# Four V projections among the first attention units, with an earlier order of turns and packed gate columns

## The chip, the cores and the metric

The kernel runs on one core of a Trainium2 chip. The metric is the device time of one execution in microseconds (us), the median of several runs. The profile is one further execution, taken by the hardware profiler. TensorE (PE) multiplies matrices, VectorE (DVE), ScalarE (ACT) and GpSimd (POOL) do the elementwise work, SyncE (SP) issues most of the DMAs. Each engine runs its own instruction stream in order; semaphores hold one stream back for another.

## The reference, cut to what matters

One decoder block on 1024 tokens of width 1024, all in float32, with 32 experts behind it:

```
h = rms_norm(x, norm_attn_g)
proj = h @ w_in                      # 3080 columns, split into:
da_q, da_k, da_v, ml_qk, ml_v, ml_o, ml_g = split(proj)
a_out = diff_attention(da_q, da_k, da_v, rel_bias_table, lam)   # 4 heads, causal
qk = silu(causal_conv(ml_qk)); gates = ml_g + mlstm_gate_b      # 4 input, 4 forget gates
m_out = mlstm_chunkwise(q, k, ml_v, log_i, log_f)               # 4 heads
m_out = head_rms_norm(m_out) * sigmoid(ml_o + mlstm_o_b)
x = x + concat(a_out, m_out) @ w_out
x = x + moe(rms_norm(x))             # top 4 of 32 experts
out = rms_norm(x, final_norm_g)
```

## The kernel before

The tokens are cut into NT = 8 tiles of 128. The kernel has five hand-written streams, one for each engine; the order of work on an engine is the order in which its code stands, and every wait is a semaphore.

**Turning x.** Each tile of x is squared (ScalarE), scaled (VectorE, L1202), turned in eight transposes on TensorE (`turn_x`, L574) and multiplied by the gain on VectorE into `hT` (L1216). Two pairs of PSUM banks alternate, so turn t waits for the gain of turn t - 2; VectorE scales tile t + 1 ahead of the gain of tile t.

**Projections.** `outs` lists 50 projections, each one bank of 128 x 512 and eight accumulating matmuls (16 passes of TensorE): QKM (8, the mLSTM's q and k), GATE (2, one for each half of the tokens, 36 columns of weights), MV (8), MO (8), Q (8), K (8), V (8). `project(o)` (L599) issues one, `take_out(o)` on ScalarE evacuates it, `proj_done` and `proj_evac` count them. Up to MO they rotate over banks 0 to 3. TensorE runs `turn_x` 0 to 3, projections 0 to 3, `turn_x` 4 to 7, the turn of the small vectors (L613), the relative-bias row (L616), and then projections 4 to 17.

**Gate rows.** The gates are scanned on VectorE (L1242) while MV runs. ScalarE computes their exponential (`em_ready`, L1036) behind its evacuation of the last MV. TensorE then transposes these rows (L625), and ahead of each of the eight MO projections it spreads half of one head's row over 128 partitions (L631, banks 6 and 7), which ScalarE copies into `m_wide`. ScalarE makes the sigmoids of the convolved q and k behind MO 4 to 7.

**mLSTM.** Eight chunks, one for each tile. Chunk t on TensorE: `ml_sums(t)` (L675, L678), a projection, `ml_chunk_state(t)` (L663), the turn of the chunk before (L686), `ml_scores(t + 1)` (L651, L655), and two more projections. So three of the 24 projections Q, K and V stand in each chunk. They and the turns share banks 6 and 7. `ml_scores(0)` stands behind all of MO. VectorE weighs scores and keys, forms queries (L1329), and divides.

**Attention.** 32 units (tile t, head h). In step u TensorE issues the transposes of unit u - 2 (L745), the logits of unit u (`da_logit`, L723, two row groups of 64 partitions), and the values of unit u - 2 (L756). Softmax runs on VectorE (L1400 to L1417) and ScalarE (L1095). In steps 4 and 6 TensorE turns the experts' bias tables (`turn_biases`, L772), from step 8 on there are output projections (L783). Banks 5 and 7 are a ring for all but the attention's own results.

**Queue of SyncE.** In its stream, `proj_done` of the last V is waited for; behind that stand the loads of the first half of w_out (over V's weights, L364), of the two bias tables `b_gu_rows` and `b_down_rows` (over `hT`, L365 and L366), of the second half of w_out (L368) and of x (L371).

**Experts.** 32 experts follow, with 4 slots of weights streamed from HBM (L923). The diff does not touch them.

Of the kernel before, what the change touches and what calls it, by code (L numbers as in the profile page):

```python
# [27 lines left out]
ACT = mybir.ActivationFunctionType  # L28
AX = mybir.AxisListType.X

P = 128
# [52 lines left out]
def build(nc, x, norm_attn_g, w_in, rel_bias_table, lambda_q1, lambda_k1, lambda_q2, lambda_k2,  # L84
# [16 lines left out]
    with ExitStack() as ctx:  # L101
# [97 lines left out]
        gd_scaled = sb("gd_scaled", [P, DAH])  # L199
        gate_bias = sb("gate_bias", [64, 1])  # L200
        neg_half = sb("neg_half", [P, NT])
# [88 lines left out]
        QKM, Q, K, V, MV, MO, GATE = range(7)  # L290
        outs = [(QKM, h, m) for h in range(2) for m in range(4)] + [(GATE, 0, 0), (GATE, 1, 0)]
        outs += [(MV, 0, t) for t in range(NT)]
# [11 lines left out]
        first_shared = after_group[MO]  # L304
        shared = []
# [3 lines left out]
        out_bank = {o: o % 4 for o in range(first_shared)}  # L309
        out_bank.update({n: 6 + j % 2 for j, (what, n) in enumerate(shared) if what == "out"})  # L310
        turn_bank = {n: 6 + j % 2 for j, (what, n) in enumerate(shared) if what == "turn"}
# [11 lines left out]
        N_SMALL = 6 + 2  # L323
        RING, END_RING = (5, 7), (0, 1, 2, 3)
        ring, ring_bank = [], {}
        ring_read = {"ml": ml_mixed, "bias": b_ready, "mix": da_mixed, "half": x1_ready,
                     "h2": h2T_ready, "logits": logits_read, "place": place_read}
# [239 lines left out]
        def _(pe):  # L567
# [10 lines left out]
            def project(o):  # L578
                kind, a, b = outs[o]
                ps_bank = bank(out_bank[o])  # L580
                if kind < 6:
                    pe.wait_ge(group_in[kind], 16)
                if kind in (QKM, Q, K, MO, GATE):
                    pe.wait_ge(hT_ready, 4 * a + 4)
                if 4 <= o < first_shared:
                    pe.wait_ge(proj_evac, o - 3)
                elif o == 0:
                    pe.wait_ge(vec_ready, 1)
                if kind == GATE:
                    pe.wait_ge(gate_w_in, 32)  # L590
                for k in range(KD):
# [28 lines left out]

            pe.wait_ge(em_ready, 1)
            pe.wait_ge(consts, 5)
            for n, row in enumerate((row_c, row_b)):
                for t in range(NT):
                    ins = pe.transpose(bank(4)[:, 32 * n + 4 * t:32 * n + 4 * t + 4], row[:, P * t:P * t + P],  # L625
                                       ident[0:MLH, 0:MLH])
            ins.then_inc(cols_ps, 1)
            for n, o in enumerate(range(after_group[MV], after_group[MO])):
# [4 lines left out]
                project(o)  # L633

            def share(j):

                if j < 2:
                    pe.wait_ge(wide_ready, 7 + j)
# [48 lines left out]

            pe.wait_ge(qk_done, 4)
            pe.wait_ge(proj_evac, first_shared)  # L690
            pe.wait_ge(v_ones, 1)
            ml_scores(0)
            for j, (what, n) in enumerate(shared):
                t = (n - first_shared) // 3 if what == "out" else n + 1
                step_out = n - first_shared - 3 * t
                if what == "out" and step_out == 0:
                    ml_sums(t)
                    share(j)
                    project(n)
                    if t < NT - 1:  # L700
                        ml_chunk_state(t)
                elif what == "turn":
                    share(j)
                    ml_turn(n, bank(turn_bank[n]))
                else:
                    if step_out == 1 and t + 1 < NT:
                        ml_scores(t + 1)
# [97 lines left out]
            def place(t):  # L805
# [154 lines left out]
        def _(act):  # L960
# [13 lines left out]
            for ap, row, n in ((norm_ffn_g, V_GF, 8), (diff_norm_g, V_GD, 4),  # L974
# [4 lines left out]
            act.wait_ge(gate_bias_clear, 1)  # L979
            act.dma_start(gate_bias[0:4, :], mlstm_gate_b[:, 0:4].rearrange("l (g o) -> (l g) o", o=1)) \  # L980
               .then_inc(small_in, 16)
            act.dma_start(gate_bias[32:36, :], mlstm_gate_b[:, 4:8].rearrange("l (g o) -> (l g) o", o=1)) \
               .then_inc(small_in, 16)
            act.dma_start(table[:, :], rel_bias_table).then_inc(table_in, 16)
# [11 lines left out]
            def take_out(o):  # L996
# [8 lines left out]
                elif kind == GATE:  # L1005
                    ins = act.activation(gate_rows[0:36, cols], ps[0:36, :], ACT.Identity, bias=gate_bias[0:36, :])
                elif kind == Q:
# [28 lines left out]
            act.activation(row_b, row_b, ACT.Exp, scale=-1.0).then_inc(em_ready, 1)  # L1036
            for n, o in enumerate(range(after_group[MV], after_group[MO])):
# [3 lines left out]
                take_out(o)  # L1041
                if n >= 4:
                    act.wait_ge(conv_done, n - 3)
                    act.activation(ml_raw[:, n - 4, :], ml_qk[:, n - 4, :], ACT.Sigmoid).then_inc(sig_done, 1)

            act.wait_ge(lam_ready, 1)
            act.activation(lam[:, 2:4], lam[:, 0:2], ACT.Exp).then_inc(lam_exp, 1)

# [23 lines left out]

            act.wait_ge(ml_fade_in, 1)
            act.activation(ml_fade[:, :, :], ml_fade[:, :, :], ACT.Exp).then_inc(ml_fade_ready, 1)
            ml_exp(0)
            ml_exp(1)
            for t in range(NT):
                if t + 1 < NT:
                    ml_fade_q(t + 1)
                if t + 2 < NT:  # L1080
                    ml_exp(t + 2)
                take_out(first_shared + 3 * t)
                if t < NT - 1:
                    ml_square(t)
                take_out(first_shared + 3 * t + 1)
                take_out(first_shared + 3 * t + 2)

# [23 lines left out]
            for u in range(len(da_units) + 2):  # L1111
# [81 lines left out]
        def _(dve):  # L1193
# [327 lines left out]
            for u in range(3, N_UNITS + 1):  # L1521
                t = u // 4 - 2
                if u in (5, 7):
                    take_biases(u // 2 - 2)
                if u % 4 == 0 and t >= 0:
# [184 lines left out]
```

## Time and profile before

| | us |
|---|---|
| median of 3 runs | 2460.75 (2460.61 to 2462.6) |
| the profiled execution | 2460.42 |
| its span, first to last instruction | 2458.7 |
| TensorE busy | 2332.1 (95%) |
| VectorE busy | 764.3 (31%) |
| ScalarE busy | 609.6 (25%) |

### The profile page before, as it was taken

Reading aid. Unit: us, or ns where it says so; the run is one execution under the profiler, and the core shown is the slowest. Engines: PE = TensorE matmul, PEld = TensorE weight load, DVE = VectorE, ACT = ScalarE, POOL = GpSimd, SP = SyncE. Lnnn points to the kernel's source line nnn. Section 1 sums busy time; section 2 is a strip of 40 time slices with the busy share of each in tenths; the row PEclk is TensorE's granted clock in tenths of the full one; section 3 lists DMA queues with packets and bytes.
Section 4 is the critical chain, followed back from the end, with each engine's and each line's share of the span. In section 5 each row is a group of like instructions: output and inputs, shape, how many; then the busy total and the mean of one; then the engine's idle time right before and its main releaser. Section 6 shows DMA issues by size and latency. Waiting matters only on the chain.

```text
span 2458.7 us, 41234 instructions
## 1 busy us (share of the span) xinstructions
PE 2332.1 (95%) x15394; PEld 1994.0 (81%) x15395; DVE 764.3 (31%) x1819; ACT 609.6 (25%) x1284; POOL 250.5 (10%) x227
## 2 busy tenths in 40 slices
PE   7999999899969999989999999999999999999994
PEld 3343545456649999989999999999999999999994
DVE  2161321477752232222323222321222222222222
ACT  2112111244402222222222222211221222222223
POOL 1000000021130111001011101100100000010011
PEclk8999999899979999999999999999999999999997
DMA  7000000211146899869889889975976788798686
GB/s 283 35 0 0 1 0 35 101 52 53 44 141 219 271 293 287 278 214 276 280 277 298 265 261 293 296 220 183 290 241 207 215 266 251 240 286 276 208 255 217
DMA packets 440328, 485.95 MB, mean 198 GB/s; under 512 B 23965, under 2 KB 417357, under 8 KB 440252
## 3 DMA queue, kind: packets, MB, share of 16 engines
q1 hardware_dynamic: 419996, 450.33, 56.1%
q0 software_dynamic: 20080, 34.88, 6.7%
q8 instruction: 28, 0.46, 0.1%
q10 hardware_dynamic: 208, 0.16, 0.0%
q14 instruction: 16, 0.13, 0.0%
HBM read 473.41 MB, written 49.58 MB: 213 GB/s over the span
## 4 chain that ended last, share of the span: by engine, by line
PE 93%; issue 2%; DVE 2%; DMA 1%; ACT 1%; POOL 0%; SPq 0%; ACTq 0%; POOLq 0%; DVEq 0%
PE PS L923 64%; PE PS L599 14%; PE PS L783 5%; PE PS L884 2%; PE PS L866 2%; PE PS L723 1%; PE PS L756 1%; PE PS L745 1%; PE PS L675 1%; PE PS L678 0%; PE PS L802 0%; DVE unit L1400 0%; PE PS L631 0%; DMA out_dram<-unit 0%; PE PS L574 0%
## 5 line engine op out<-in xcount | busy, mean ns | idle before, releaser
L923 PE MATMUL PS<-pairA,unit 128*128 x12288 | 1588.1, 291 | 25.9 <-issue 23.3
L923 PEld LDWEIGHTS PS<-pairA,unit 128*128 128x128 f32 x12288 | 1561.7, 191 | 45.0 <-issue 34.5
L599 PE MATMUL PS<-pairA,unit 128*128 128x512 f32 (+1 forms) x544 | 245.4, 609 | 2.5 <-issue 2.5
L1646 DVE TENSOR_SCALAR unit<-PS,cur_b 128x256 f32<-128x256 f32 x256 | 112.1, 479 | 368.4 <-PE PS L923 353.5
L1178 ACT ACTIVATE unit<-PS,cur_b 128x256 f32<-128x256 f32 x256 | 107.5, 471 | 457.0 <-PE PS L923 457.0
L599 PEld LDWEIGHTS PS<-pairA,unit 128*128 128x128 f32 (+1 forms) x544 | 101.9, 191 | 138.2 <-issue 137.6
L1165 ACT ACTIVATE unit<-unit 128x512 f32<-128x512 f32 x128 | 80.6, 630 | 482.1 <-DVE unit L1646 470.0
L1169 ACT ACTIVATE unit<-PS,cur_b 128x256 f32<-128x256 f32 x256 | 107.5, 471 | 321.4 <-PE PS L923 321.4
L517 POOL DMA_INDIRECT unit<-h_dram,cur_x x66 | 69.5, 1053 | 1011.1 <-DVE cur_x L1640 994.6
L1653 DVE TENSOR_SCALAR unit<-unit 128x512 f32<-128x512 f32 x128 | 54.7, 427 | 344.8 <-ACT unit L1169 344.8
L536 POOL DMA_INDIRECT acc_dram<-pairA,cur_y x66 | 105.9, 1604 | 531.7 <-ACT pairA L1149 521.0
L1638 DVE COPY cur_b<-b_all 128x24 f32 x32 | 5.7, 178 | 436.0 <-ACT unit L1178 433.8
L1651 DVE TENSOR_TENSOR unit<-unit 128x512 f32<-128x512 f32 x128 | 88.7, 693 | 89.1 <-ACT unit L1165 89.1
L599 PE MATMUL PS<-unit,pairA 128*128 128x512 f32 x256 | 111.4, 594 | 0.2 <-ACT unit L1015 0.2
L599 PEld LDWEIGHTS PS<-unit,pairA 128*128 128x128 f32 x256 | 48.1, 190 | 60.0 <-issue 59.2
L1655 DVE SCALAR_TENSOR_TENSOR pairA<-unit 128x512 f32<-128x512 f32 x128 | 88.6, 693 | 4.4
L1616 DVE TENSOR_TENSOR pairA<-PS,vec 128x512 f32<-128x512 f32 x132 | 81.9, 682 | 0.4 <-PE PS L866 0.3
L1149 ACT ACTIVATE pairA<-PS,g_now 128x512 f32<-128x512 f32 x132 | 80.3, 700 | 6.6 <-PE PS L884 6.6
L866 PE MATMUL PS<-ident,unit 128*128 128x128 f32 x384 | 48.7, 278 | 19.7 <-DMA unit<-h_dram,cur_x 19.7
L1095 ACT ACTIVATE unit<-unit,small 128x128 f32<-128x128 f32 (+7 forms) x64 | 49.4, 772 | 54.4 <-DVE small L1403 51.0
L866 PEld LDWEIGHTS PS<-ident,unit 128*128 128x128 f32 x384 | 44.7, 144 | 20.0 <-issue 19.8
L783 PE MATMUL PS<-unit,pairA 128*128 128x512 f32 x128 | 58.4, 599 | 0.0
(228 smaller groups left out, 1245.2 us busy)
## 6 DMA issues: line engine op xcount, KB each, us to landing
unit<-in_expert_w_gu_dram SPq DMA_DIRECT2D x256, 1024.0 KB, 5.3
unit<-in_expert_w_down_dram SPq DMA_DIRECT2D x128, 1024.0 KB, 6.7
unit<-in_w_in_dram SPq DMA_DIRECT2D x6, 2048.0 KB, 14.5
pairB<-in_x_dram SPq DMA_DIRECT2D x16, 512.0 KB, 9.9
unit<-in_w_out_dram SPq DMA_DIRECT2D x2, 2048.0 KB, 12.0
h_dram<-pairA SPq DMA_DIRECT2D x8, 512.0 KB
acc_dram<-pairB SPq DMA_DIRECT2D x8, 512.0 KB
pairB<-acc_dram SPq DMA_DIRECT2D x8, 512.0 KB, 6.4
```

Of the source, the lines that this page charges most:

```text
L536: pool.indirect_dma_start(out=acc_dram, out_offset=bass.IndirectOffsetOnAxis(ap=cur_y[:, b:b + 1], axis=0), in_=y_rows[:, b, :], in_offset ...
L599: ins = pe.matmul(ps, lhs, rhs, start=(k == 0), stop=(k == KD - 1))
L783: ins = pe.matmul(ps, (da_mixT, ml_mixT)[k // 4][:, k % 4, P * t:P * t + P], w_o[k // 4][:, k % 4, HALF * half:HALF * half + HALF], start= ...
L866: ins = pe.transpose(bank(4 + q)[:, 256 * k + P * b:256 * k + P * b + P], xg[:, b, P * (2 * q + k):P * (2 * q + k) + P], ident[:, :])
L923: ins = pe.matmul(bank(s)[:, ITEM * j:ITEM * j + w], slot_w[s][:, k, P * j:P * j + P], xa_cols[:, ITEM * k:ITEM * k + KD * ITEM + w][:, ba ...
L1165: act.activation(glu_s[:, c % 2, :], glu_t[:, c % 2, :], ACT.Sigmoid, scale=ALPHA).then_inc(sig_ready, 1)
L1169: ins = act.activation(lin_b[:, c % 2, ITEM * j:ITEM * j + ITEM], bank(up_slot)[:, ITEM * j:ITEM * j + ITEM], ACT.Identity, bias=cur_b[:, ...
L1178: ins = act.activation(yT[:, 2 * s + j, :], bank(s)[:, ITEM * j:ITEM * j + ITEM], ACT.Identity, bias=cur_b[:, 2 * NF + 2 * s + j:2 * NF + ...
L1616: dve.tensor_tensor(xT[:, 2 * q:2 * q + 2, :], kn(bank(4 + q), 2), wide(vec[:, V_GF + 2 * q:V_GF + 2 * q + 2], ITEM), ALU.mult).then_inc(r ...
L1646: ins = dve.tensor_scalar(glu_t[:, c % 2, ITEM * j:ITEM * j + ITEM], bank(gate_slot)[:, ITEM * j:ITEM * j + ITEM], cur_b[:, 2 * c + j:2 * ...
L1651: step.do(dve.tensor_tensor(glu_s[:, c % 2, :], glu_t[:, c % 2, :], glu_s[:, c % 2, :], ALU.mult))
L1655: dve.scalar_tensor_tensor(out=actT[:, 2 * c:2 * c + 2, :].rearrange("p j n -> p (j n)"), in0=lin_c[:, c % 2, :], scalar=1.0, in1=glu_s[:, ...
```

## The change

- `turn_x` 4, 5 and 6, 7 move among projections 0 to 3: turn 4 behind projection 0, turn 5 behind 1, turns 6 and 7 behind 2.
- GATE becomes one out. For each k two matmuls with the same 36 columns of weights: the first half of the tokens goes to partitions 0 to 35 of the bank, the second to 64 to 99. ScalarE evacuates both; `gate_bias` is held at four places, so two more DMAs are issued.
- The transposes of the gate rows follow MO 0; the widenings are issued in pairs behind MO 0 to 3, the sigmoids of q and k follow them; `ml_scores(0)` stands between MO 6 and MO 7, and on ScalarE the fades and `ml_exp` 0 and 1 ahead of the evacuation of MO 7. MO 6 and 7 use banks 6 and 7.
- Chunks 4 to 7 hold two projections each, not three. The last four V projections (tiles 4 to 7) are issued in steps 0 to 3 of the attention, behind the logits, in the ring of banks 5 and 7. ScalarE evacuates each behind the exponentials of its unit.
- The bias tables are turned in steps 5 and 7, and taken in 6 and 8. SyncE's code is unchanged: its wait for the last V now means the one in step 3.

```diff
-        outs = [(QKM, h, m) for h in range(2) for m in range(4)] + [(GATE, 0, 0), (GATE, 1, 0)]
+        outs = [(QKM, h, m) for h in range(2) for m in range(4)] + [(GATE, 0, 0)]
...
+        LATE_V = 4
+        shared, chunk_outs = [], []
         for t in range(NT):
-            o = first_shared + 3 * t
-            shared += [("out", o)] + ([("turn", t - 1)] if t else []) + [("out", o + 1), ("out", o + 2)]
+            o = first_shared + (3 * t if t < 4 else 2 * t + 4)
+            chunk_outs.append(range(o, o + (3 if t < 4 else 2)))
+            shared += [("out", o)] + ([("turn", t - 1)] if t else []) + [("out", n) for n in chunk_outs[t][1:]]
...
                     elif kind == GATE:
-                        ps, lhs, rhs = ps_bank[0:36, :], gate_w[:, k, :], hT[:, k, HALF * a:HALF * a + HALF]
+                        pe.matmul(ps_bank[0:36, :], gate_w[:, k, :], hT[:, k, 0:HALF], start=(k == 0), stop=(k == KD - 1))
+                        ps, lhs, rhs = ps_bank[64:100, :], gate_w[:, k, :], hT[:, k, HALF:SEQ]
...
             for o in range(4):
                 project(o)
-            for t in range(4, NT):
-                turn_x(t)
+                if o < 3:
+                    turn_x(4 + o)
+                if o == 2:
+                    turn_x(NT - 1)
...
-            pe.wait_ge(qk_done, 4)
-            pe.wait_ge(proj_evac, first_shared)
+            for n, o in enumerate(range(after_group[MV], after_group[MO])):
+                if n >= 6:
+                    pe.wait_ge(wide_ready, n + 1)
+                project(o)
+                if n == 0:
+                    turn_gate_rows()
+                if n < 4:
+                    widen(2 * n)
+                    widen(2 * n + 1)
+                if n == 6:
+                    pe.wait_ge(qk_done, 4)
+                    pe.wait_ge(proj_evac, first_shared - 3)
+                    ml_scores(0)
+            pe.wait_ge(proj_evac, first_shared - 2)
             pe.wait_ge(v_ones, 1)
-            ml_scores(0)
...
-                    pe.wait_ge(proj_evac, N_OUTS)
+                    pe.wait_ge(proj_evac, N_OUTS - LATE_V)
...
+            def late_values(u):
+                o = N_OUTS - LATE_V + u
+                next_bank("v", o)
+                out_bank[o] = ring_bank["v", o]
+                project(o)
+
+            u = 0
             da_logit(0)
+            late_values(0)
             da_logit(1)
+            late_values(1)
             for u in range(2, N_UNITS + 2):
...
                 if u < N_UNITS:
                     da_logit(u)
+                if u < LATE_V:
+                    late_values(u)
                 if len(da_groups[u - 2]) > 1:
                     da_turn_weights(u - 2, 1)
-                if u in (4, 6):
-                    turn_biases(u // 2 - 2)
+                if u in (5, 7):
+                    turn_biases((u - 5) // 2)
...
+            for n, o in enumerate(range(after_group[MV], after_group[MO])):
+                if n == 7:
+                    act.wait_ge(lam_ready, 1)
+                    act.activation(lam[:, 2:4], lam[:, 0:2], ACT.Exp).then_inc(lam_exp, 1)
+                    act.wait_ge(ml_fade_in, 1)
+                    act.activation(ml_fade[:, :, :], ml_fade[:, :, :], ACT.Exp).then_inc(ml_fade_ready, 1)
+                    ml_exp(0)
+                    ml_exp(1)
+                take_out(o)
+                if n < 4:
+                    take_wide(2 * n)
+                    take_wide(2 * n + 1)
+                    act.wait_ge(conv_done, n + 1)
+                    act.activation(ml_raw[:, n, :], ml_qk[:, n, :], ACT.Sigmoid).then_inc(sig_done, 1)
...
+                if u < LATE_V:
+                    take_out(N_OUTS - LATE_V + u)
```

## Rows read from the trace of the kernel before

**Rows 1.** The page, chain that ended last, shares of the span by line
```profile
PE PS L923 64%; PE PS L599 14%; PE PS L783 5%; PE PS L884 2%; PE PS L866 2%; PE PS L723 1%; PE PS L756 1%; PE PS L745 1%; PE PS L675 1%; PE PS L678 0%; PE PS L802 0%; DVE unit L1400 0%; PE PS L631 0%; DMA out_dram<-unit 0%; PE PS L574 0%
```
**Rows 2.** Windows by stage: length, busy time of each engine, granted clock, DMA share, GB/s
```profile
49.80:63.80 14.00, 8.77 (x39) 4.64 (x37) 7.71 (x18) 1.19 (x2) 2.97 (x8) 0.70 0.03 10
...
163.00:168.30 5.30, 2.25 (x20) 1.32 (x19) 0.00 (x0) 2.94 (x3) 0.00 (x0) 0.96 0.00 0
...
233.70:242.10 8.40, 3.93 (x20) 3.33 (x20) 5.89 (x20) 6.64 (x12) 0.00 (x0) 0.65 0.00 0
242.10:447.40 205.30, 205.05 (x621) 102.27 (x619) 47.08 (x124) 34.71 (x109) 7.83 (x7) 1.00 0.03 11
447.40:475.50 28.10, 21.10 (x95) 13.68 (x94) 20.10 (x88) 13.26 (x57) 2.02 (x2) 0.57 0.63 220
475.50:700.00 224.50, 219.29 (x1061) 133.12 (x1059) 152.58 (x465) 87.74 (x223) 39.42 (x41) 1.00 0.13 48
```
**Rows 3.** Chain of waits in an mLSTM chunk: start, length, what
```profile
382.69 13.73 PE PS L599 x32
```
**Rows 4.** Chain of waits, the head of the kernel
```profile
19.95 29.99 PE PS L599 x64
49.94 0.89 PE PS L574 x8
...
60.31 3.50 PE PS L616 x4
63.81 99.22 PE PS L599 x224
```
**Rows 5.** Timeline of VectorE, last scaling ahead of projection 0's end
```profile
20.57 0.75 DVE L1202 TENSOR_SCALAR pairB<-pairB,rstd 128x1024 f32<-128x1024 f32 x1 [0.67 <-POOL rstd L458]
```
**Rows 6.** Timeline of the gate projections: 24 passes, and a weight load
```profile
97.42 10.46 PE L599 MATMUL PS<-pairA,unit 128*36 128x512 f32 x24
...
97.43 0.11 PEld L599 LDWEIGHTS PS<-pairA,unit 128*36 128x36 f32 x1 [0.32 <-issue]
```
**Rows 7.** Chain of waits, logits of a unit of the last tile
```profile
645.30 1.94 PE PS L723 x8
```
**Rows 8.** Chain of waits from the end of MV into the first chunk
```profile
166.07 1.15 PE PS L625 x16
...
176.90 1.05 PE PS L631 x2
177.95 7.06 PE PS L599 x16
...
240.02 2.09 PE PS L675 x8
242.11 7.37 PE PS L599 x16
...
250.35 0.65 PE PS L651 x8
```
**Rows 9.** Timeline of VectorE in the same chunk as rows 3
```profile
385.46 0.42 DVE L1329 TENSOR_TENSOR unit<-unit,pairB 128x256 f32<-128x256 f32 x1
```
**Rows 10.** Timeline of TensorE in the first attention units
```profile
448.19 0.49 PE L723 MATMUL PS<-pairB,unit 64*128 64x128 f32 x4 [0.78 <-ACT unit L1015]
...
460.86 1.91 PE L772 MATMUL PS<-ident,pairA 32*128 32x32 f32 x16
...
464.79 0.79 PE L756 MATMUL PS<-unit 128*128 128x128 f32 x2
...
475.52 0.70 PE L783 MATMUL PS<-unit,pairA 128*128 128x512 f32 x1
```
**Rows 11.** Timeline of SyncE: issue of the gate/up bias rows
```profile
447.87 0.51 SPq L365 DMA_DIRECT2D pairA<-in_expert_b_gu_dram  x1
```
**Rows 12.** Landing of that DMA (L365), counted from its issue
```profile
DMA to landing us min/median/max: 10.6/10.6/10.6
```
**Rows 13.** Landing of the second half of w_out (L368), from its issue
```profile
DMA to landing us min/median/max: 14.9/14.9/14.9
```

More of the change, by code:

```diff
@@ L199, in build @@
         gd_scaled = sb("gd_scaled", [P, DAH])
-        gate_bias = sb("gate_bias", [64, 1])
+        gate_bias = sb("gate_bias", [P, 1])
         neg_half = sb("neg_half", [P, NT])
@@ L304, in build @@
         first_shared = after_group[MO]
-        shared = []
+        LATE_V = 4
+        shared, chunk_outs = [], []
         for t in range(NT):
-            o = first_shared + 3 * t
-            shared += [("out", o)] + ([("turn", t - 1)] if t else []) + [("out", o + 1), ("out", o + 2)]
+            o = first_shared + (3 * t if t < 4 else 2 * t + 4)
+            chunk_outs.append(range(o, o + (3 if t < 4 else 2)))
+            shared += [("out", o)] + ([("turn", t - 1)] if t else []) + [("out", n) for n in chunk_outs[t][1:]]
+        step_of = {n: (t, k) for t, ns in enumerate(chunk_outs) for k, n in enumerate(ns)}
         out_bank = {o: o % 4 for o in range(first_shared)}
+        out_bank.update({first_shared - 2: 6, first_shared - 1: 7})
         out_bank.update({n: 6 + j % 2 for j, (what, n) in enumerate(shared) if what == "out"})
@@ L322, in build @@
         N_UNITS = len(da_units)
-        N_SMALL = 6 + 2
+        N_SMALL = 6 + 4
         RING, END_RING = (5, 7), (0, 1, 2, 3)
         ring, ring_bank = [], {}
-        ring_read = {"ml": ml_mixed, "bias": b_ready, "mix": da_mixed, "half": x1_ready,
+        ring_read = {"v": proj_evac, "ml": ml_mixed, "bias": b_ready, "mix": da_mixed, "half": x1_ready,
                      "h2": h2T_ready, "logits": logits_read, "place": place_read}
@@ L582, in project @@
                     pe.wait_ge(group_in[kind], 16)
-                if kind in (QKM, Q, K, MO, GATE):
+                if kind in (QKM, Q, K, MO):
                     pe.wait_ge(hT_ready, 4 * a + 4)
@@ L590, in project @@
                     pe.wait_ge(gate_w_in, 32)
+                    pe.wait_ge(hT_ready, NT)
                 for k in range(KD):
@@ L619, in _, with turn_gate_rows, widen @@
                 project(o)
[L621 to L628, printed above, removed]
+            def turn_gate_rows():
+                pe.wait_ge(em_ready, 1)
+                pe.wait_ge(consts, 5)
+                for n, row in enumerate((row_c, row_b)):
+                    for t in range(NT):
+                        ins = pe.transpose(bank(4)[:, 32 * n + 4 * t:32 * n + 4 * t + 4], row[:, P * t:P * t + P],
+                                           ident[0:MLH, 0:MLH])
+                ins.then_inc(cols_ps, 1)
+            def widen(n):
                 if n >= 2:
@@ L632, in _ @@
                           start=True, stop=True).then_inc(wide_ps, 1)
-                project(o)
             def share(j):
                 if j < 2:
-                    pe.wait_ge(wide_ready, 7 + j)
+                    pe.wait_ge(proj_evac, first_shared - 1 + j)
                 elif shared[j - 2][0] == "out":
@@ L687, in ml_turn @@
                 ins.then_inc(ml_turned, 1)
-            pe.wait_ge(qk_done, 4)
-            pe.wait_ge(proj_evac, first_shared)
+            for n, o in enumerate(range(after_group[MV], after_group[MO])):
[12 more added lines that the diff above has]
+            pe.wait_ge(proj_evac, first_shared - 2)
             pe.wait_ge(v_ones, 1)
-            ml_scores(0)
             for j, (what, n) in enumerate(shared):
-                t = (n - first_shared) // 3 if what == "out" else n + 1
-                step_out = n - first_shared - 3 * t
+                t, step_out = step_of[n] if what == "out" else (n + 1, None)
                 if what == "out" and step_out == 0:
@@ L979, in _ @@
             act.wait_ge(gate_bias_clear, 1)
[L980 to L983, printed above, removed]
+            for lo, c in ((0, 0), (32, 4), (64, 0), (96, 4)):
+                act.dma_start(gate_bias[lo:lo + 4, :], mlstm_gate_b[:, c:c + 4].rearrange("l (g o) -> (l g) o", o=1)) \
+                   .then_inc(small_in, 16)
             act.dma_start(table[:, :], rel_bias_table).then_inc(table_in, 16)
@@ L1005, in take_out @@
                 elif kind == GATE:
-                    ins = act.activation(gate_rows[0:36, cols], ps[0:36, :], ACT.Identity, bias=gate_bias[0:36, :])
+                    act.activation(gate_rows[0:36, 0:HALF], ps[0:36, :], ACT.Identity, bias=gate_bias[0:36, :])
+                    ins = act.activation(gate_rows[0:36, HALF:SEQ], ps[64:100, :], ACT.Identity, bias=gate_bias[64:100, :])
                 elif kind == Q:
@@ L1036, in _, with take_wide @@
             act.activation(row_b, row_b, ACT.Exp, scale=-1.0).then_inc(em_ready, 1)
-            for n, o in enumerate(range(after_group[MV], after_group[MO])):
+            def take_wide(n):
                 act.wait_ge(wide_ps, n + 1)
@@ L1040, in _ @@
                                ACT.Copy).then_inc(wide_ready, 1)
[L1041 to L1047, printed above, removed]
             def ml_square(t):
@@ L1071, in ml_fade_q @@
                 ins.then_inc(ml_qd_ready, 1)
[L1073 to L1076, printed above, removed]
+            for n, o in enumerate(range(after_group[MV], after_group[MO])):
[12 more added lines that the diff above has]
+                    act.activation(ml_raw[:, n, :], ml_qk[:, n, :], ACT.Sigmoid).then_inc(sig_done, 1)
             for t in range(NT):
@@ L1081, in _ @@
                     ml_exp(t + 2)
[L1082 to L1086, printed above, removed]
+                for n in chunk_outs[t]:
+                    take_out(n)
+                    if n == chunk_outs[t][0] and t < NT - 1:
+                        ml_square(t)
             def da_exps(u):
@@ L1522, in _ @@
                 t = u // 4 - 2
-                if u in (5, 7):
-                    take_biases(u // 2 - 2)
+                if u in (6, 8):
+                    take_biases((u - 6) // 2)
                 if u % 4 == 0 and t >= 0:
```

## The prediction

> **What bounds the kernel now.** I read the page's chain of waits first: TensorE is on it nearly all the time, two thirds of it in the experts' matmuls (L923), and 14% in the input projections (L599) [rows 1]. The change touches nothing behind the attention, so I cut the part ahead of it with the windows view [rows 2]. A stage matters here by its gaps and its clock: 49.8 to 63.8 us has TensorE busy 8.8 of 14.0 us at a granted clock of 0.70; 163.0 to 168.3 has 2.3 of 5.3; 233.7 to 242.1 has 3.9 of 8.4 at 0.65; 447.4 to 475.5 has 21.1 of 28.1 at 0.57. The mLSTM loop between, 242.1 to 447.4, is full (205.1 of 205.3), as is the attention behind 475.5. So the change can win in four holes, and in the full stretch only by taking matmuls out. A projection at the full clock is worth half of two in a row, 13.73 / 2 = 6.87 us [rows 3].
>
> **Part 1, turns among the first four projections.** Now the four projections run 19.95 to 49.94, then turns 4 to 7, each behind a scaling on VectorE that itself waits for the turn before, then the gain rows and the relative-bias row, and projection 4 starts at 63.81 [rows 4]. Gap 13.9 us. Afterwards turn 4 runs behind projection 0; its tile is scaled long before (the scaling at 20.57 is already that of tile 5 [rows 5]); VectorE has 6.87 us for what each later turn needs, against about 3 us that turn, gain and scaling take. What remains: four turns at 0.89, about 0.3 for the gain rows, the four bias-row passes at full clock 3.50 / 2 = 1.75, some 0.3 for changing over: 5.9 us. Saved 8.0. Bounds: 8 if the clock loss stays, 11. The two more gate-bias DMAs cost ScalarE's queue two more issues, ahead of squares that wait for rows of x anyway: nothing, up to 0.7 us were they exposed.
>
> **Part 2, gate columns.** Now the two gate outs are 16 passes each with 36 columns of weights, at 0.429 us a pass (24 of them in 10.46) [rows 6], 13.7 us. Afterwards the same 32 passes are issued, one half of the tokens into partitions 0 to 35, the other into 64 to 99. No row of before shows two column groups side by side. The nearest row is the attention's logits, two row groups of 64: eight passes of 512 columns in 1.94 us, where serial passes would need 3.43 [rows 7]. Two groups run together there, with about 0.2 us of start. I take that: 32 passes in about 7.3, saved 6.4 us. Bounds 0 (no overlap) and 6.9. The gate rows' scan on VectorE starts about 0.7 us later behind the projection, since both halves are now evacuated after it; the eight MV projections (55 us) cover it, and what lies behind em is hidden by part 3.
>
> The Trainium skill says the same of column groups as of rows ("TensorEngine Tiling (Array Packing)", Key Properties: tiles execute loads and matmuls in parallel, a change of mode drains the engine). But "TensorE: Matmul & The Clock Gate", What overlaps and what doesn't, says a weight load overlaps with running matmuls only where the row group differs, and here the row groups are the same. By the first the sum stands; by the second it is the rival with exposed loads below. No row of before decides between them.
>
> **Part 3, MO stage.** Now from the end of MV (163.0) to the first shared projection (242.11) 79.1 us pass. In it: the wait for em 3.0; the transposes 1.15; eight times a widening (1.05) and a projection (7.06), a pair 8.11, where 2 x 0.43 + 6.87 = 7.73, so each insertion costs 0.38 of change-over; a half-clock start of 1.5; then 6.3 us from MO 7 until the sums, with qk, fades and ml_exp(0) in line, and sums at half clock, 2.09 [rows 8]. Afterwards projection MO 0 goes ahead of the em wait. ScalarE needs 0.6 + 1.28 + 1.05, about 3 us, for em behind the last MV: hidden in 6.87. The eight widenings go in four pairs; qk is complete after MO 3, ml_scores(0) goes between MO 6 and MO 7, and the fades and ml_exp(0) (some 3 us on ScalarE) lie under MO 7. What remains: 8 x 6.87 = 55.0; transposes 1.15; 16 widening passes 6.9; four insertions 1.5; scores 1.0 (0.65 for eight of their ten passes [rows 8]); sums 2.09 / 2 = 1.05. Total 66.6, saved 12.5, and 0.3 of half-clock time in the first shared projection (7.37 against 7.06). Sum 12.8. Bounds 10 (one of the hidden chains 3 us late) and 14 (pairs without any change-over).
>
> **Part 4, four V projections moved.** Out of the mLSTM loop go 4 x 6.87 = 27.5 us. Does a chunk with one projection behind its scores still keep up? In a chunk of before the scores end at 382.69, VectorE has weights, keys and queries for the next sums ready at 385.46 + 0.42 = 385.9 [rows 3, 9], and one projection runs until 389.6. Slack 3.7 us, so nothing is given back there.
>
> Into the attention's first units go the same 27.5. Now from the last V (447.4) to the first output projection 28.1 us pass, mostly chains over VectorE and ScalarE at the half clock [rows 2, 10]. Afterwards, counted from the end of the last V in the loop: its evacuation and issue 0.75; logits 0 to 3 at 0.49, 2.0 [rows 10]; four projections 27.5; transposes, values and the last mLSTM turn among them about 1.1: the last V ends at 31.3. The softmax chains of units 0 to 3 are hidden under them. But SyncE holds the loads of both halves of w_out, of both bias tables and of x behind that last V, since these tiles lie over V's weights and hT. Now the gate/up bias rows land 0.43 + 10.6 = 11.0 us behind the last V, and turn_biases(0) starts at 460.86, 13.4 behind it, so the load is just hidden [rows 10 to 12]. Afterwards turn_biases(0), although a unit later (u = 5), is reached about 4.5 us behind the last V: TensorE stands about 6.5 us, and everything in its order (values 3, logits 6) stands behind it, then VectorE and ScalarE. So: 31.3 + 11.0, biases 1.9 (at half clock again, as now), then from values 3 to the output projection as now, 475.52 - 464.79 = 10.7 [rows 10]. Total 54.9, added 26.8. Net gain of part 4 only 0.7 us: what the cover wins, the wait for the bias rows takes. Bounds: a loss of 2.7 if the half clock afterwards reaches over half of the first output projection (3.4 us), a gain of 8 if the bias wait did not show (below).
>
> **Sum.** 10.8 + 6.4 + 12.8 + 0.7 = 30.7 us. The profiled execution took 2460.42 (span 2458.7); 2429.7. The median of the runs is 0.33 above it: 2430.0.
>
> **Rivals.**
> *Column groups do not overlap.* Nothing else changes; against it only the row of the row groups [rows 7]. 2430.0 + 6.4 = 2436.4. Chance 0.17.
> *Their weight loads show.* 32 loads of 0.11 us [rows 6] uncovered, 3.5 us: 2433.5. Chance 0.10. It is the Trainium skill's sentence on row groups that speaks for it.
> *The bias rows are not waited for*, for example because they land early. Then the second half of w_out decides: issued 1.4 us behind the last V, landing 14.9 later, 16.3 [rows 13]. The output projection would start at 31.3 + 16.3 = 47.6, 7.3 us sooner: 2422.7. Against it: the bias rows queue behind 2 MB in the same queue and their 10.6 us will hardly shrink. Chance 0.07.
> *Slower: the clock stays low.* Behind the bias wait TensorE would stay at 1.2 GHz into the full stretch from 475.5 on. Each us of full-clock work there costs one more at half, so it decides from about 31 us of such work (62 us at half clock). Now the clock is back at the first output projection and the stretch from 475.5 runs at 1.00 [rows 2]. Chance 0.03.
> *No change.* The holes close but the attention takes them back, being bound by VectorE; against it, VectorE is busy only 152.6 of 224.5 us there, TensorE 219.3 [rows 2]. 2460; chance 0.02.
> My forecast keeps 0.61.
>
> **How the numbers follow.** Likeliest 2430.0. The range reaches to the early-bias case below (2422) and past the no-overlap case above with part 4's loss half in it (2438); outside are 0.08 or so. Within 0.2% (about 5 us, what a measurement of this kernel can tell from no change) only the last rival lies; slower by more than that only the clock rival. Faster 0.95, same 0.02, slower 0.03.
>
> **What the profile after would show.** Between projections 3 and 4 about 2.4 us of other matmuls at clock 1.00, the turns singly among the first four. The gate's passes with 36 columns: 32 in about 7.3 us (13.7: no overlap; about 10.8: loads). ACT's em exponential under MO 0, scores between MO 6 and 7, sums right behind MO 7, some 66.6 us behind MV. Chunks 4 to 7 about 19.4 us apart, without idle time. In the attention four V projections at the full clock, then TensorE standing 6 to 7 us ahead of the bias transposes, released by a DMA, and the first output projection about 23.6 us behind the last V. The first two are independent of the rest; the forecast fails most easily in the gate's overlap and in the bias wait.

## The result

| | us |
|---|---|
| before, median of 4 runs | 2460.68 (2459.67 to 2462.6) |
| after, median of 4 runs | 2431.75 (2430.13 to 2433.48) |
| ratio, with its 95% interval | 0.9882 (0.9865 to 0.9899) |
| the profiled execution, before and after | 2460.42 and 2430.13 |
| its span, before and after | 2458.7 and 2428.4 |

The change makes the kernel 1.2% faster; the forecast was 2430.0 in a range of 2422 to 2438.

### The profile after

The windows view by stage (length; busy time and count of TensorE, its weight loads, VectorE, ScalarE, GpSimd; granted clock; DMA share; GB/s) answers to [rows 2]:

```profile
19.00:52.00 33.00, 32.60 (x96) 16.08 (x96) 8.08 (x15) 3.82 (x7) 3.52 (x9) 1.00 0.93 332
52.00:54.30 2.30, 2.30 (x7) 0.41 (x6) 0.84 (x6) 1.19 (x2) 0.00 (x0) 1.00 0.00 0
54.30:144.00 89.70, 89.70 (x226) 38.33 (x226) 47.65 (x61) 13.07 (x18) 0.00 (x0) 1.00 0.06 24
144.00:210.40 66.40, 66.40 (x180) 29.28 (x179) 9.98 (x24) 22.37 (x31) 0.00 (x0) 1.00 0.00 0
210.40:387.70 177.30, 177.05 (x556) 89.88 (x555) 47.09 (x124) 35.57 (x110) 7.83 (x7) 1.00 0.04 12
387.70:419.40 31.70, 30.92 (x91) 14.48 (x91) 8.39 (x43) 7.46 (x30) 1.01 (x1) 1.00 0.00 0
419.40:431.00 11.60, 2.18 (x14) 1.04 (x13) 3.23 (x16) 3.19 (x11) 0.00 (x0) 0.77 0.90 274
431.00:443.30 12.30, 11.48 (x57) 8.35 (x57) 8.53 (x29) 5.17 (x20) 1.01 (x1) 0.52 0.60 244
443.30:668.00 224.70, 219.49 (x1062) 133.33 (x1062) 152.76 (x465) 87.76 (x223) 39.42 (x41) 1.00 0.14 49
```

Three of the four holes of [rows 2] are gone: from projection 0 to the end of the mLSTM TensorE is busy at a clock of 1.00. The fourth has moved and changed its cause: behind the last late V projection (419.4) TensorE works 2.2 of 11.6 us while the DMA engines are 90% busy, and the clock has fallen to half behind it.

The chain of waits (start, length, what; L578 is `turn_x`, L624 the relative-bias row, L634 the gate rows' transposes, L641 the widenings, L659 the scores, L605 the projections, L790 the turn of the experts' bias tables) answers to [rows 3, 4, 8]:

```profile
19.40 8.85 PE PS L605 x16
28.25 0.87 PE PS L578 x8
...
52.54 1.80 PE PS L624 x4
54.34 27.66 PE PS L605 x64
...
151.00 1.08 PE PS L634 x16
152.08 1.82 PE PS L641 x4
153.90 7.07 PE PS L605 x16
...
201.62 0.65 PE PS L659 x8
...
210.39 6.87 PE PS L605 x16
...
353.61 7.06 PE PS L605 x16
...
419.84 11.16 DMA pairA<-in_expert_b_gu_dram
431.05 1.91 PE PS L790 x16
```

Turn 4 stands right behind projection 0, and projection 4 starts at 54.34 where it started at 63.81. The rows' transposes start with no wait at 151.00, behind MO 0. The DMA of the gate/up bias rows is now a link of the chain, 11.16 us long, where before it had only just been hidden.

The timeline of TensorE in the gate projection and in the first attention units (start, length, engine, line, idle time before and its releaser) answers to [rows 6, 10]:

```profile
82.39 0.59 PE L600 MATMUL PS<-pairA,unit 128*36 128x512 f32 x1
82.40 0.59 PE L605 MATMUL PS<-pairA,unit 128*36 128x512 f32 x1
82.83 0.59 PE L600 MATMUL PS<-pairA,unit 128*36 128x512 f32 x1
82.83 0.59 PE L605 MATMUL PS<-pairA,unit 128*36 128x512 f32 x1
...
88.93 3.27 PE L605 MATMUL PS<-unit,pairA 128*128 128x512 f32 x7
...
412.25 7.13 PE L605 MATMUL PS<-unit,pairA 128*128 128x512 f32 x16
...
421.71 0.70 PE L741 MATMUL PS<-pairB,unit 64*128 64x256 f32 x4 [0.83 <-DVE small L1437]
431.05 1.91 PE L790 MATMUL PS<-ident,pairA 32*128 32x32 f32 x16 [8.64 <-DMA pairA<-in_expert_b_gu_dram]
...
443.23 1.98 PE L801 MATMUL PS<-unit,pairA 128*128 128x512 f32 x4
```

The two column groups start within 0.01 us of each other, a pair each 0.43 us: the gate takes 7.0 us, 81.94 to 88.93. The last late V projection ends at 419.4; TensorE reaches the bias turn at about 422.4 and stands 8.64 us for a DMA.

### The profile page after: what moved, and what is told of

Same layout as the page of the kernel before. It is cut to its first block, busy times and chain, and to the rows that moved or that the text cites. A ratio compares the mean times of both kernels' runs of the same rounds, so it can differ in the third digit from the quotient of the medians.

```text
span 2428.4 us, 41240 instructions
## 1 busy us (share of the span) xinstructions
PE 2312.1 (95%) x15394; PEld 1988.9 (82%) x15395; DVE 764.5 (31%) x1819; ACT 612.6 (25%) x1286; POOL 250.6 (10%) x227
## 4 chain that ended last, share of the span: by engine, by line
PE 94%; issue 2%; DMA 2%; DVE 1%; ACT 1%; POOL 0%; SPq 0%; ACTq 0%; POOLq 0%; DVEq 0%
PE PS L952 65%; PE PS L605 14%; PE PS L801 5%; PE PS L913 2%; PE PS L895 2%; PE PS L774 1%; PE PS L741 1%; PE PS L763 1%; PE PS L686 0%; PE PS L683 0%; DMA pairA<-in_expert_b_gu_dram 0%; PE PS L820 0%; PE PS L641 0%; PE PS L578 0%; DMA out_dram<-unit 0%
## 5 line engine op out<-in xcount | busy, mean ns | idle before, releaser
L605 PE MATMUL PS<-pairA,unit 128*128 128x512 f32 (+1 forms) x528 | 233.4, 598 | 2.0 <-issue 2.0
L605 PEld LDWEIGHTS PS<-pairA,unit 128*128 128x128 f32 (+1 forms) x528 | 97.9, 189 | 119.9 <-issue 119.2
L605 PE MATMUL PS<-unit,pairA 128*128 128x512 f32 x256 | 112.3, 596 | 0.3 <-ACT unit L1044 0.3
L605 PEld LDWEIGHTS PS<-unit,pairA 128*128 128x128 f32 x256 | 47.9, 190 | 59.1 <-issue 57.8
L895 PEld LDWEIGHTS PS<-ident,unit 128*128 128x128 f32 x384 | 44.9, 144 | 19.9 <-issue 19.8
```

Of the source, the lines that this page charges most:

```text
L895: ins = pe.transpose(bank(4 + q)[:, 256 * k + P * b:256 * k + P * b + P], xg[:, b, P * (2 * q + k):P * (2 * q + k) + P], ident[:, :])
```

## The experiments

Each ran beside the kernel before on the same chip, whose own median lay between 2460.97 and 2462.29. The ratio's interval is some 0.14% wide to either side, about 3.3 us, and differences between two changed kernels are compared across such groups; smaller ones are read from the stages of the traces.

| label | median us | ratio to before, 95% interval |
|---|---|---|
| e1_turns_alone | 2452.47 | 0.9963 (0.9950 to 0.9977) |
| e2_gate_blocks | 2436.38 | 0.9898 (0.9883 to 0.9913) |
| e3_no_late_v | 2431.71 | 0.9877 (0.9862 to 0.9892) |
| e4_biases_later | 2425.45 | 0.9850 (0.9836 to 0.9863) |
| e5_biases_ahead | 2422.90 | 0.9842 (0.9829 to 0.9856) |
| e6_ahead_six_late | 2418.20 | 0.9830 (0.9816 to 0.9843) |
| e7_rows_apart | 2430.45 | 0.9868 (0.9853 to 0.9883) |
| e8_ahead_apart | 2420.81 | 0.9833 (0.9819 to 0.9846) |
| e9_six_apart | 2417.58 | 0.9824 (0.9811 to 0.9838) |
| e10_seven_apart | 2421.09 | 0.9838 (0.9824 to 0.9851) |
| e11_rows_first | 2435.19 | 0.9895 (0.9880 to 0.9910) |

### e1_turns_alone: part 1 by itself

```diff
 # the kernel before
             for o in range(4):
                 project(o)
-            for t in range(4, NT):
-                turn_x(t)
+                if o < 3:
+                    turn_x(4 + o)
+                if o == 2:
+                    turn_x(NT - 1)
```

> The kernel before with the early order of the turns alone. Theory: the hole ahead of projection 4 goes and with it the half-clock start behind it; projection 4 starts at about 54.9 where it started at 63.8, the 14 projections take 96.4 where they took 99.2, together 11.5 us: 2449.2. Rival: part of these 12 us of the changed kernel came from the gate columns or a luckier start of projection 0 (0.55 us earlier there), and the turns give 8 to 9 alone: 2452.

Measured 9.8 us below the kernel before that ran beside it (2462.29). The chain of waits of this kernel:

```profile
20.07 9.01 PE PS L599 x16
...
53.37 1.80 PE PS L618 x4
55.17 96.66 PE PS L599 x224
```

Projection 4 starts 8.6 us sooner than in [rows 4] and the 14 projections take 2.6 us less: 11.2 us in the stage, as the theory had it. The median, 2452.5, is nearer to the rival's 2452 than to 2449.2; its interval (5.7 to 12.3 us gained) holds both. The rival's reason, that the stage gives less than 11, is refuted by the rows. The profiled span of e1 is only 9.1 us shorter (2449.6), since some 2 us are lost again behind the attention, as in the changed kernel (last part of the next section).

### e2_gate_blocks: what makes column groups overlap

```diff
 # the changed kernel
+                if kind == GATE:
+                    for k in range(KD):
+                        pe.matmul(ps_bank[0:36, :], gate_w[:, k, :], hT[:, k, 0:HALF], start=(k == 0), stop=(k == KD - 1))
                 for k in range(KD):
...
                     elif kind == GATE:
-                        pe.matmul(ps_bank[0:36, :], gate_w[:, k, :], hT[:, k, 0:HALF], start=(k == 0), stop=(k == KD - 1))
                         ps, lhs, rhs = ps_bank[64:100, :], gate_w[:, k, :], hT[:, k, HALF:SEQ]
```

> The changed kernel, with the 16 gate passes of the first column group issued as one block and the 16 of the second behind it, where they alternated by two. Theory: matmuls start in the order of issue, so two column groups only overlap where passes of different groups stand next to each other; here only at the seam: the gate takes 13.3 us in place of 7.0, 2431.75 + 6.3 = 2438. Rival: an idle column group takes its passes from further back in the queue: no change, 2431.8.

Measured 2436.38. Timeline of TensorE (L598 the first group, L607 the second and all other projections):

```profile
82.68 5.77 PE L598 MATMUL PS<-pairA,unit 128*36 128x512 f32 x13
87.86 0.62 PE L607 MATMUL PS<-pairA,unit 128*36 128x512 f32 x1
88.28 0.59 PE L598 MATMUL PS<-pairA,unit 128*36 128x512 f32 x1
88.32 0.59 PE L607 MATMUL PS<-pairA,unit 128*36 128x512 f32 x1
...
89.18 5.74 PE L607 MATMUL PS<-pairA,unit 128*36 128x512 f32 x13
94.85 3.70 PE L607 MATMUL PS<-unit,pairA 128*128 128x512 f32 x8
```

The first line ends at 88.45, so the last of its thirteen passes, of 0.59 us, starts at 87.86, and the second group's first pass starts beside it. So twelve passes of the first group run alone, four stand beside four of the second, twelve of the second run alone: 12.2 us for the same 32 passes (28 times 0.43 is 12.0), against 7.0. The gain of part 2 comes from the overlap and needs passes of both groups close together in the queue. The theory's strict order of issue is not borne out: the second group's first pass started ahead of three passes of the first that were issued before it, which is why the gate takes 12.2 us and not 13.3. It ran ahead by no more than that; the rival falls.

### e3_no_late_v: part 4 undone

```diff
 # the changed kernel
-        LATE_V = 4
+        LATE_V = 0
...
-            o = first_shared + (3 * t if t < 4 else 2 * t + 4)
-            chunk_outs.append(range(o, o + (3 if t < 4 else 2)))
+            o = first_shared + (3 * t if t < 8 else 2 * t + 8)
+            chunk_outs.append(range(o, o + (3 if t < 8 else 2)))
...
-            late_values(0)
...
-            late_values(1)
...
-                if u in (5, 7):
-                    turn_biases((u - 5) // 2)
+                if u in (4, 6):
+                    turn_biases((u - 4) // 2)
```

(`take_biases` on VectorE moves from steps 6 and 8 to 5 and 7 with it.)

> The changed kernel with all V projections back in the mLSTM chunks (three in each) and the bias tables turned in steps 4 and 6; parts 1 to 3 stay. Theory: the late V projections cover the softmax chains of the first units, but the bias rows are then waited for and take the gain back; within 1 us of the changed kernel, 2432.3. Rival: the move is worth the 7 us that the chains of units 0 to 3 took: 2439.

Measured 2431.71, the changed kernel's 2431.75 within a tenth, closer than the runs can tell apart. The stage says it better: from the first shared projection (210.99) to the first output projection (443.74) this kernel takes 232.75 us, the changed kernel 232.84 (210.39 to 443.23):

```profile
429.23 1.91 PE L790 MATMUL PS<-ident,pairA 32*128 32x32 f32 x16
...
443.74 3.70 PE L801 MATMUL PS<-unit,pairA 128*128 128x512 f32 x8
```

No DMA is named ahead of the bias turn here: the bias rows, issued at 416.24, land 10.0 us later, 3 us before it. The four late V projections, the part that names the change, are worth nothing as the change places them; the rival (2439) falls.

### e4_biases_later: the wait given other work

```diff
 # the changed kernel
-                if u in (5, 7):
-                    turn_biases((u - 5) // 2)
+                if u in (7, 9):
+                    turn_biases((u - 7) // 2)
...
-                if u in (6, 8):
-                    take_biases((u - 6) // 2)
+                if u in (8, 10):
+                    take_biases((u - 8) // 2)
```

> The changed kernel with the bias tables turned in steps 7 and 9 and taken in 8 and 10, loads untouched. Theory: TensorE works through units 5 and 6 while the bias rows land, reaches the turn about 9.5 us behind the last V with 1.5 to 2 us left to wait, and the first output projection starts about 17 us behind the last V where it took 23.9: 2431.75 - 6.5 = 2425. Rival: the units behind the wait are bound by their own chains over VectorE and ScalarE, or the second half of w_out (16.3 behind the last V) is what the output projection then waits for longer: no more than 2 us, 2430.

Measured 2425.45, 6.3 us below the changed kernel. In the trace the first output projection starts at 441.35, 16.6 us behind the end of the last V (424.79), where it was 23.8. The DMA is not named at all; what is waited for are the softmax chains:

```profile
432.89 1.20 PE L774 MATMUL PS<-unit 128*128 128x128 f32 x4 [2.08 <-ACT unit L1147]
...
435.60 1.91 PE L790 MATMUL PS<-ident,pairA 32*128 32x32 f32 x16
```

This profiled execution is 5.4 us late at the last V, for a reason that has nothing to do with the edit: its projection 0 starts 1.4 us later and runs 0.7 longer, and its clock falls in the MO stage (below).

### e5_biases_ahead: the wait removed at its source

```diff
 # the changed kernel
-        b_gu_rows = pairA[0:N_EXP, 4096:6144]
+        b_gu_rows = pairB[0:N_EXP, 0:2048]
-        b_down_rows = pairA[0:N_EXP, 6144:7168]
+        b_down_rows = pairB[0:N_EXP, 3072:4096]
...
-            sp.wait_ge(proj_done, after_group[V])
-            sp.dma_start(w_o[0], w_out_k[:, 0:4, :]).then_inc(w_out_in0, 16)
+            sp.wait_ge(ml_h_done, NT)
             sp.dma_start(b_gu_rows, expert_b_gu.rearrange("l e f -> (l e) f")).then_inc(b_gu_in, 16)
             sp.dma_start(b_down_rows, expert_b_down.rearrange("l e d -> (l e) d")).then_inc(b_down_in, 16)
-            sp.wait_ge(ml_h_done, NT)
             sp.dma_start(w_o[1], w_out_k[:, 4:8, :]).then_inc(w_out_in1, 16)
...
-            for t in range(3):
+            load_x_again(2)
+            sp.wait_ge(proj_done, after_group[V])
+            sp.dma_start(w_o[0], w_out_k[:, 0:4, :]).then_inc(w_out_in0, 16)
+            sp.wait_ge(b_turned, 1)
+            for t in range(2):
                 load_x_again(t)
```

> The changed kernel with the bias rows held in other tiles (over the mLSTM's q and k and the square's tile), so that they and the second half of w_out are loaded behind the last mLSTM sums, ahead of the late V projections; behind the last V only the first half of w_out is left, and two of the three first x tiles, which wait for the first bias turn. Turns in steps 5 and 7 as in the changed kernel. Theory (the wait for the bias rows is what took the gain): no DMA wait ahead of the bias turn, the first output projection about 15.5 us behind the last V where it took 23.9, 2431.75 - 8.4 = 2423.3. Rival (the chains of units 4 to 8 over VectorE and ScalarE bind, the wait only covered them): 17 us or more as in the run with the turns two steps later, 2425 to 2426.

Measured 2422.90, 8.9 us below the changed kernel. Timeline of SyncE, and of TensorE:

```profile
373.90 0.33 SPq L368 DMA_DIRECT2D pairB<-in_expert_b_gu_dram  x1
...
420.45 0.37 SPq L377 DMA_DIRECT2D unit<-in_w_out_dram  x1
```

```profile
423.38 1.18 PE L792 MATMUL PS<-ident,pairB 32*128 32x32 f32 x16
...
428.53 1.19 PE L776 MATMUL PS<-unit 128*128 128x128 f32 x4 [2.08 <-ACT unit L1149]
...
436.12 4.13 PE L803 MATMUL PS<-unit,pairA 128*128 128x512 f32 x8
```

The bias turn comes 2.9 us behind the last V (420.45) with no wait, the first output projection 15.7 us behind it. That names the wait as what took part 4's gain. Not run were the loads ahead without the late V projections; in e3 nothing up to the first output projection waits for a DMA, which argues that they would win nothing there, but does not show it. The chains of the units are the next limit (2.08 us for ScalarE), as the rival says, but not the only one.

### e6_ahead_six_late and e10_seven_apart: how far the cover reaches

```diff
 # e5_biases_ahead; e10 has 7, and 1 in place of 2, and e7's edit too
-        LATE_V = 4
+        LATE_V = 6
...
-            o = first_shared + (3 * t if t < 4 else 2 * t + 4)
-            chunk_outs.append(range(o, o + (3 if t < 4 else 2)))
+            o = first_shared + (3 * t if t < 2 else 2 * t + 2)
+            chunk_outs.append(range(o, o + (3 if t < 2 else 2)))
```

> As e5_biases_ahead, with six V projections late (steps 0 to 5) and two projections in chunks 2 to 7. Theory: two more projections cover the idle time of units 4 and 5, and the first half of w_out (about 10 us behind the last V) is not waited for long: up to 3.5 us below e5_biases_ahead, 2420. Rival: with the last V only three units ahead of the first output projection, the load of w_out is waited for, and the gain goes there: 2423 to 2425. A chunk with two projections keeps up in both.

> As e9_six_apart with seven late V projections (steps 0 to 6, two projections in chunks 1 to 7). Theory: the first half of w_out can only be issued behind the last V and lands 8 to 9 us later, while two units of 5 to 6 us are left to work on; TensorE waits 2 to 3 us for a DMA ahead of the first output projection, which takes back what the cover of unit 6 wins: 2418, within 1 us of e9_six_apart. Rival: the cover of unit 6 is worth more than the wait: 2415.5.

Six late: 2418.20, 4.7 below e5_biases_ahead and better than the theory's 2420; the output projection starts at 432.97, 11.1 us behind the last V. Seven late: 2421.09, and its timeline shows the turning point:

```profile
434.50 5.40 PE L803 MATMUL PS<-unit,pairA 128*128 128x512 f32 x8 [3.78 <-DMA unit<-in_w_out_dram]
```

The first half of w_out is issued at 426.75, behind the last V, and lands 7.7 us later; TensorE waits 3.78 us for it and its clock falls (5.40 us for the eight passes that take 3.70 with six late). The theory had 2418 for seven and 2 to 3 us of wait; it is 3.5 us worse than six, so the wait and the clock behind it cost more than was put down.

### e7_rows_apart, e8_ahead_apart, e9_six_apart: the clock in the MO stage

```diff
 # the changed kernel (e7), e5_biases_ahead (e8), e6_ahead_six_late (e9); ScalarE's side likewise
-                if n < 4:
-                    widen(2 * n)
-                    widen(2 * n + 1)
+                if 1 <= n < 5:
+                    widen(2 * n - 2)
+                    widen(2 * n - 1)
```

> The changed kernel with the four pairs of widenings behind MO 1 to 4, so that a full projection stands between the 16 small transposes of the gate rows and the first pair. 
> Both edits together, of e5_biases_ahead and of e7_rows_apart. Theory: their gains add, 2422. Rival: as e5_biases_ahead.

> Six late V projections and the loads ahead (as e6_ahead_six_late), with the widenings behind MO 1 to 4 (as e7_rows_apart). Theory: the sparse passes no longer let the clock fall in some executions, 0.5 to 1 us below the 2418.2 of e6_ahead_six_late and a spread under 3 us: 2417.5. Rival: as e6_ahead_six_late, with single executions 3 to 5 us above the rest.

Why the edit: in two of the six traces with the rows' transposes and the first widenings both behind MO 0 (changed kernel, e2 to e6), the clock falls there though TensorE has no idle time. Chain of waits and windows of e4_biases_later:

```profile
153.06 1.08 PE PS L634 x16
154.13 2.29 PE PS L641 x4
156.43 9.94 PE PS L605 x16
```

```profile
154.00:156.00 2.00, 2.00 (x7) 0.64 (x5) 0.00 (x0) 0.60 (x1) 0.00 (x0) 0.84 0.00 0
156.00:158.00 2.00, 2.00 (x3) 0.84 (x3) 0.00 (x0) 1.53 (x2) 0.00 (x0) 0.50 0.00 0
```

The same projection takes 9.94 us where it takes 7.07 in the changed kernel's own trace. With the widenings apart none of four traces (e7 to e10) shows a fall in this stage. The medians move by 1.3 (e7), 2.1 (e8 below e5) and 0.6 us (e9 below e6), all downward, each inside the interval; e7's spread, 2427.9 to 2432.3, did not shrink, e8's did (2420.0 to 2422.2 against 2419.6 to 2425.6). Four traces against two falls in six settle nothing, so whether the order prevents the fall stays open. e9_six_apart is the fastest version, 2417.58.

### e11_rows_first: the em wait put back

```diff
 # the changed kernel
-                project(o)
                 if n == 0:
                     turn_gate_rows()
+                project(o)
```

> The changed kernel with the transposes of the gate rows ahead of MO 0 again, the widenings behind MO 0 as changed. Theory: the wait for em of 3.0 us comes back, and with it a half-clock start worth 1.6 us: 2431.75 + 4.6 = 2436.3. Rival: the clock falls at the rows in any case, so only the wait comes back: 2434.8.

Measured 2435.19, 3.4 above the changed kernel, between the two numbers. The timeline decides:

```profile
148.01 1.15 PE L634 MATMUL PS<-ident,pairB 4*128 4x4 f32 x16 [3.06 <-ACT pairB L1065]
149.09 8.83 PE L605 MATMUL PS<-pairA,unit 128*128 128x512 f32 x16
```

Both are back: a wait of 3.06 us for ScalarE and a projection of 8.8 us in place of 7.1, 4.8 us in the stage. The theory stands there; the medians cannot tell 4.6 from 3.0.

## Why the prediction was right, point by point

| term | predicted gain | traces, before to after |
|---|---|---|
| part 1, turns | 10.8 | 9.5 (63.81 to 54.34) + 2.8 (clock) = 12.3 |
| part 2, gate columns | 6.4 | 13.7 to 7.0 = 6.7 |
| part 3, MO stage | 12.8 | 79.1 to 66.4, and 0.3 = 13.0 |
| part 4, late V | 0.7 | -27.6 in the chunks, +27.4 in the attention: 0.2 |
| sum | 30.7 | 32.2 at the first output projection |
| behind it | 0 | -1.9 |
| span | 30.7 | 30.3 |

The mechanism of all four parts was right. That 30.7 came so near to 30.3 is partly luck: the stages gave 1.5 us more than forecast, and 1.9 us that the sum does not have were lost behind the attention.

**Part 1** was right in its mechanism and 1.5 us small: 0.55 is an earlier start of projection 0 (19.40 against 19.95), which e1_turns_alone (20.07) shows to be chance; the first four projections take 29.5 us where they took 30.0, and what stands between them 5.5 us where 5.9 were forecast. By itself the part gives 11.2 us in the stage.

**Part 2**: the row of the row groups [rows 7] held for column groups. Of the two sentences of the Trainium skill that stood against each other, the trace sides with "TensorEngine Tiling (Array Packing)", Key Properties. The loads of 0.11 us, which by the Trainium skill's "TensorE: Matmul & The Clock Gate", What overlaps and what doesn't, should have shown in one row group, did not: 32 passes took 7.0 us. The rivals of no overlap and of exposed loads are refuted.

**Part 3**: 66.6 us predicted from the end of MV to the first shared projection, 66.4 measured. An insertion costs its 0.38 us of change-over as before (1.91 + 7.06 = 8.97, against 4 x 0.43 + 6.87 = 8.59), now four times.

**Part 4**: chunks 4 to 7 lose exactly their projection (353.61 is 19.4 us behind 334.21), with no idle time: the slack was there. In the attention the last V ends 31.7 us behind the loop (31.3 predicted), the bias rows land 11.6 behind it (11.0), and from there it is 12.3 us to the output projection (12.6). TensorE's idle time ahead of the bias turn was 8.64, not 6.5, since it came there sooner, 3.0 us behind the last V and not 4.5; as the landing sets the end, this changes nothing. e3 shows the net of zero, e5 that the wait is its cause. The rival that the bias rows are not waited for was priced at 7.3 us, with the second half of w_out as the next limit; e5, which removes the wait and loads that half early as well, gains 8.2 in the stage (23.8 to 15.7).

**The slower rival**: the half clock had ended when the first output projection started, as before; the stretch behind it runs at 1.00. The 224.7 us of that stretch answer to the 224.5 of [rows 2], so the holes' gain was not taken back either.

**What was not foreseen**: 1.9 us are lost behind the attention. Up to the first expert's matmuls nothing is lost (443.30 to 697.63, 254.3 us, as before). The experts' first 128 passes then take 18.16 us where they took 15.94 before, but that is not the loss: in the kernel before it is the second 128 passes that are slow. Chain of waits of the kernel before, then of the changed one:

```profile
753.78 18.20 PE PS L923 x128
...
1052.50 19.90 PE PS L923 x128
```

```profile
697.63 18.16 PE PS L952 x128
...
1020.60 21.35 PE PS L952 x128
```

The second 128 passes of the changed kernel take 15.94, and the third 128 start 298.2 us behind the first output projection in both kernels. The loss comes later. Behind a stretch in which TensorE has little work (busy 0.86 of the 5.60 us before 1020.60), 128 passes take 21.35 us in the changed kernel, from 1020.60, and 19.90 in the kernel before, from 1052.50; counted from the first output projection they also start 0.3 us later (577.3 for 577.0). The granted clock in their first 4.4 us is 0.50, and 0.86 in the 5 us behind; in the kernel before it is 0.68 in the first 4.5 us and then 1.00. The twelve other traces run the same experts' code: these passes take 19.9 to 20.0 us in six of them (the kernel before, e2, e4, e6, e9, e10) and 21.2 to 21.5 in six (e1, e3, e5, e7, e8, e11). From the first output projection to the end they take between 1982.9 us (e8) and 1986.1 (e3). So the change itself is not shown to cost these 1.9 us; what decides when the clock rises there stays open, and a difference of some 3 us between two single traces can come from behind the attention.

## What to carry to other kernels

When work moves past a point that a DMA queue waits for, the loads behind that point move too: price the consumer's new distance from them, and give the tiles a place that frees them earlier. Filling an idle stage with moved matmuls is worth only what the next wait leaves; here the move was worth nothing as it stood, and the kernel got 8.9 us faster once the loads no longer stood behind it; too much of it (seven projections) gave part back. Narrow matmuls into different column groups run side by side if their passes stand close together in the queue.

## What the runs showed of the hardware

- Two column groups with 36 columns of float32 weights each, over the same 128 rows: a pair of passes every 0.43 us, starts 0.01 us apart, loads hidden. In two blocks of 16 passes only four pairs overlap at the seam, 12.2 us against 7.0; there the second block's first pass starts ahead of three passes that were issued before it.
- TensorE's granted clock fell from 2.4 to 1.2 GHz while the engine was busy without a gap, 2.00 of 2.00 us, with 16 transposes of 4x4 and four passes of 4 rows behind them, in two of six traces; the projection behind took 8.8 and 9.9 us for 7.1. A busy TensorE row is not proof of the full clock.
- 256 KB of bias rows queued behind a 2 MB load land 10.6 us (before) and 11.16 us (after) behind their issue. Issued with no large load ahead of them in e5, the same rows land 3.3 us behind it; it is the place in the queue, not their size, that has to be priced.
